# One 512-column product for a weight's upper part in the last feed-forward block of a two-model kernel

## The reference, cut to what matters

```
def sqrelu_mlp(hn, w1, w2):
    return jnp.square(jax.nn.relu(hn @ w1)) @ w2        # w1: 1024 x 4096, w2: 4096 x 1024

    hn = modulate_2(rms_norm_2(h, norm2_g[layer]), sh2, sc2)
    h = h + g2[:, None, :] * sqrelu_mlp(hn, mlp_w1[layer], mlp_w2[layer])
```

## Time and profile before

| What | Value |
|---|---|
| median of 3 runs | 1750.71 us (1750.46 to 1750.80) |
| the profiled execution, its own time | 1754.25 us |
| its span in the profile | 1752.4 us |
| mean granted TensorE clock | 0.988 of full speed |
| TensorE busy | 1679.9 us, 96% |
| VectorE busy | 1285.6 us, 73% |
| ScalarE busy | 822.3 us, 47% |
| GpSimd busy | 242.1 us, 14% |
| transfers | 317.86 MB, mean 181 GB/s |

### The profile page before, as it was taken

The page is one execution under the profiler, slowest core; times in us unless marked ns, Lnnn a source line. Parts: engine busy times, 40 slices in busy tenths (PEclk is TensorE's granted clock), DMA queues, the critical chain, the costliest instruction groups (busy, mean ns, idle before and its releaser), DMA issues.

```text
span 1752.4 us, 28651 instructions
## 1 busy us (share of the span) xinstructions
PE 1679.9 (96%) x11826; PEld 1508.6 (86%) x11826; DVE 1285.6 (73%) x1777; ACT 822.3 (47%) x1186; POOL 242.1 (14%) x199
## 2 busy tenths in 40 slices
PE   6999999999999999999999999969999999899999
PEld 3797778788788876987999999969999999799999
DVE  4667863887888878866478777887988868757453
ACT  3433662543224423646464555575635445456362
POOL 0323001011001112440310121013000220030000
PEclk9899999999999999999999999989999999999999
DMA  8644002243465558320346656634998966137552
GB/s 303 264 169 168 1 1 96 77 158 117 169 238 205 186 192 324 122 73 1 100 168 247 215 200 251 214 120 160 360 364 322 345 217 227 38 121 283 186 180 73
DMA packets 46577, 317.86 MB, mean 181 GB/s; under 512 B 5232, under 2 KB 6256, under 8 KB 12272
## 3 DMA queue, kind: packets, MB, share of 16 engines
q1 hardware_dynamic: 45936, 312.68, 49.4%
q0 software_dynamic: 512, 3.35, 0.5%
HBM read 314.96 MB, written 1.05 MB: 180 GB/s over the span
## 4 chain that ended last, share of the span: by engine, by line
PE 82%; DVE 10%; ACT 3%; issue 2%; POOL 2%; DMA 1%; DVEq 0%; ACTq 0%
PE PM L1619 22%; PE PM L1620 22%; PE PM L1621 22%; PE PO L1934 3%; PE PM L1894 2%; DVE wlo L1021 2%; PE PX L1918 2%; DVE acc L1055 1%; PE PX L1803 1%; PE PX L1592 1%; PE PX L1860 1%; DVE Hlo L1517 1%; PE PM L1703 1%; PE PX L1966 1%; PE PM L1705 1%
## 5 line engine op out<-in xcount | busy, mean ns | idle before, releaser
L1619 PE MATMUL PM<-Hhi,whi 128*128 128x256 f32 (+1 forms) x1686 | 526.9, 313 | 6.5 <-DVE Hlo L1443 2.0
L1620 PE MATMUL PM<-Hlo,whi 128*128 128x256 f32 (+1 forms) x1686 | 523.4, 310 | 0.0
L1621 PE MATMUL PM<-Hhi,wlo 128*128 128x256 f32 (+1 forms) x1686 | 523.3, 310 | 0.0
L1021 DVE TENSOR_TENSOR wlo<-raw,whi 128x2048 fp32r<-128x2048 f32 (+2 forms) x199 | 437.9, 2200 | 93.8 <-ACT whi L721 93.4
L721 ACT ACTIVATE whi<-raw 128x2048 fp32r<-128x2048 f32 (+3 forms) x204 | 365.5, 1792 | 141.8 <-PE PM L1621 91.3
L1619 PEld LDWEIGHTS PM<-Hhi,whi 128*128 128x128 f32 x1686 | 323.7, 192 | 30.1 <-issue 8.9
L1621 PEld LDWEIGHTS PM<-Hhi,wlo 128*128 128x128 f32 x1686 | 323.8, 192 | 16.4
L1620 PEld LDWEIGHTS PM<-Hlo,whi 128*128 128x128 f32 x1686 | 323.9, 192 | 15.9
L1619 PE MATMUL PM<-Ghi,whi 128*128 128x256 f32 (+1 forms) x864 | 265.1, 307 | 1.7 <-DVE X L1202 1.6
L1621 PE MATMUL PM<-Ghi,wlo 128*128 128x256 f32 (+1 forms) x864 | 263.2, 305 | 0.0
L1620 PE MATMUL PM<-Glo,whi 128*128 128x256 f32 (+1 forms) x864 | 263.2, 305 | 0.0
(11 more groups left out here) (222 smaller groups left out, 2276.4 us busy)
## 6 DMA issues: line engine op xcount, KB each, us to landing
raw<-in_ada SPq DMA_DIRECT2D x104, 1024.0 KB, 5.1
raw<-in_wm SPq DMA_DIRECT2D x93, 1024.0 KB, 5.5
raw<-in_wl SPq DMA_DIRECT2D x68, 1024.0 KB, 4.9
raw<-in_wl SPq DMA_DIRECT2D x32, 704.0 KB, 4.2
raw<-in_wm SPq DMA_DIRECT2D x5, 768.0 KB, 4.4
raw<-in_wm SPq DMA_DIRECT2D x4, 704.0 KB, 4.2
X<-in_x SPq DMA_DIRECT2D x1, 2048.0 KB, 10.9
bias<-in_bias POOLq DMA_DIRECT2D x1, 2048.0 KB, 9.8
```

What stands on the lines that cost most here:

```text
L1021: dve.tensor_tensor(wslot(wlo, i, usize(u)), slot_raw(n, usize(u)), wslot(whi, i, usize(u)).bitcast(F32), ALU.subtract)\
L1619: pe.matmul(out, st_hi, mv_hi, start=first, stop=False)
L1620: pe.matmul(out, st_hi, mv_lo, start=False, stop=False)
L1621: return pe.matmul(out, st_lo, mv_hi, start=False, stop=last)
```

## The change

It applies to 31 of the 32 MLP units of stage M1: all `w2` units and all `w1` units but index 0 (unit 172 runs in another order, with the norm before it). `Hhi` and `Hlo` become two halves of one buffer `H2`, `Ghi` and `Glo` of one buffer `G2`. For each weight block there are now two matrix multiplications: `whi` with a moving operand of two pieces of 256 columns, the upper and the lower part of the activation, into all 512 columns of a bank; and `wlo` with the upper part, 256 columns, added to the first half of that bank. The two halves of the bank are added when it is evacuated:

- `w1`: ScalarE copies the second halves to `T` (semaphore `low`); VectorE adds the first halves from PSUM (`pm_dve`), then makes max(r, 0) * r (`silu_dve`), then runs `split_lo(i + 2)`, which stood ahead of the evacuation; ScalarE makes the rounding copy into `Ghi`, VectorE the `Glo` subtraction as before.
- `w2`: VectorE does X = second half * gate + X, waits for that instruction to end, and then X = first half * gate + X.

```
+        H2 = sb("H2", 2 * KD * 512, F32R)
+        Hhi, Hlo = H2[:, 0:KD * 512], H2[:, KD * 512:2 * KD * 512]
...
+        G2 = sb("G2", 2 * HALF * 512, F32R, reg0)
+        Ghi, Glo = G2[:, 0:HALF * 512], G2[:, HALF * 512:2 * HALF * 512]
...
+        def wide(u):
+            return u["st"] == "M1" and (u["kind"] == "w2" or u["kind"] == "w1" and u["idx"] > 0)
+
+        def both_parts(u, k):
+            buf, n = (G2, HALF * 512) if u["kind"] == "w2" else (H2, KD * 512)
+            return view(buf[:, :], "p (h c) -> p h c", h=2, c=n)[:, :, k * 256:k * 256 + 256]
...
@@ ScalarE, evacuation of w1
+                    if wide(u):
+                        act.activation(view(r, "p (c t) -> p c t", c=2), view(pm(i, 0, 1024), "p (c t) -> p c t", c=2)[:, :, 256:512],
+                                       ACT.Copy).then_inc(*tick("low", i))
+                        act.wait_ge(*at("silu_dve", i))
+                        k = u["idx"] % 8
+                        act.activation(Ghi[:, k * 512:k * 512 + 512], g, ACT.Copy).then_inc(*tick("ghi", i))
+                        return
@@ VectorE, residual
+                    if wide(u):
+                        dst = X[:, c * 512:c * 512 + 256]
+                        link(dve.scalar_tensor_tensor(out=dst, in0=pm(i, 256, 256), scalar=modc(v, 0, c), in1=dst, op0=ALU.mult, op1=ALU.add))
@@ VectorE, evacuation of w1
+                    if wide(u):
+                        r, g = tslot(2 * (i % 2)), tslot(2 * (i % 2) + 1)
+                        dve.wait_ge(*at("low", i))
+                        dve.tensor_tensor(view(r, "p (c t) -> p c t", c=2), view(pm(i, 0, 1024), "p (c t) -> p c t", c=2)[:, :, 0:256],
+                                          view(r, "p (c t) -> p c t", c=2), ALU.add).then_inc(*tick("pm_dve", i))
+                        dve.wait_ge(*at("pm_dve", i))
+                        dve.scalar_tensor_tensor(out=g, in0=r, scalar=0.0, in1=r, op0=ALU.max, op1=ALU.mult).then_inc(*tick("silu_dve", i))
+                        split_lo(i + 2)
@@ VectorE, a step
-                    if (u["kind"], u["idx"]) != ("lpart", 0) and not soon:
+                    if (u["kind"], u["idx"]) != ("lpart", 0) and not soon and not (u["kind"] == "w1" and wide(u)):
                         split_lo(i + 2)
@@ TensorE, unit
+                elif wide(u):
+                    for c in range(u["cols"] // 128):
+                        for k in range(kt):
+                            if c == 0:
+                                operand_ready(u, k)
+                            w0 = k * u["cols"] + c * 128
+                            pe.matmul(view(pm(i, c * 512, 512), "p (h t) -> p h t", h=2), wslot(whi, i, 128, w0), both_parts(u, k),
+                                      start=(k == 0), stop=False)
+                            ins = pe.matmul(pm(i, c * 512, 256), wslot(wlo, i, 128, w0), mh[:, k * S:k * S + 256], start=False, stop=(k == kt - 1))
```

More of the change, by code:

```diff
@@ L346, in noted @@
         return self.known.get((name, key), 0)
-SEMAPHORES = ["small", "x_in", "hi", "lo", "raw_used", "raw_split", "unit", "pm_act", "pm_dve", "aux", "aux_act", "aux_dve",
+SEMAPHORES = ["small", "x_in", "hi", "lo", "low", "silu_dve", "raw_used", "raw_split", "unit", "pm_act", "pm_dve", "aux", "aux_act", "aux_dve",
               "silu_c", "mod", "sq", "sqadd", "sumsq", "sd", "rinv", "rspread", "xr", "hhi", "hlo", "xres",
@@ L377, in build @@
         X = sb("X", KD * 512)
-        Hhi = sb("Hhi", KD * 512, F32R)
-        Hlo = sb("Hlo", KD * 512, F32R)
+        H2 = sb("H2", 2 * KD * 512, F32R)
+        Hhi, Hlo = H2[:, 0:KD * 512], H2[:, KD * 512:2 * KD * 512]
         T = sb("T", 4 * 512)
@@ L382, in build @@
         cursor[0] += 2 * HALF * 512 * 4
-        Ghi = sb("Ghi", HALF * 512, F32R, reg0)
-        Glo = sb("Glo", HALF * 512, F32R, reg0 + HALF * 512 * 4)
+        G2 = sb("G2", 2 * HALF * 512, F32R, reg0)
+        Ghi, Glo = G2[:, 0:HALF * 512], G2[:, HALF * 512:2 * HALF * 512]
         zu = sb("zu", 2048, F32, reg0)
```

## The result

| | before | after |
|---|---|---|
| median of six runs each | 1750.59 us (1749.38 to 1752.94) | 1756.72 us (1754.38 to 1758.81) |
| ratio | | 1.0028, 95% interval 1.0017 to 1.0039 |
| the profiled execution, its span | 1754.25, 1752.4 us | 1756.82, 1755.0 us |
| unit 173's first product to the end of the span | 182.9 us | 188.3 us |
| TensorE, VectorE, ScalarE busy | 1679.9, 1285.6, 822.3 us | 1675.5, 1311.2, 813.1 us |

What follows compares the result with a forecast made beforehand. TensorE was taken as the bound, with VectorE nearly full for some 25 us. -6.6 + 6.0 + 1.0 + 0.5 + 1.7 = +2.6 us on the profiled 1754.25; median forecast 1753.3 us, range 1748.8 to 1757.0.

Steps and rivals of the forecast that it cites:

- two-piece rival: 512-column multiplication in each of 496 blocks: two-piece stream costs up to 13.3 ns a block more, 1758.8 us; chance 0.14.
- VectorE beside the ada parts: Steps 173 to 176: VectorE cycles of 6.66 or 6.96 us against TensorE's 5.55; stalls together +6.0 us.
- Stalls of 0.2, 1.4 and 4.4: TensorE waits for split_lo(176), for split_lo(177), and at the 16 sums behind unit 177 for ada part 103.
- cheap-VectorE rival: VectorE's two new instructions at 0.40 us each, so part 103 ends 2.3 us earlier: 1748.3 us; chance 0.12.
- The saving of 6.6 us: TensorE, 496 blocks of 31 units: 512 plus 256 columns take 0.3467 instead of 0.360 us, 13.3 ns less each.
- The clock: TensorE behind the 4.4 us pause: one fall of the clock to half speed, +1.7 us.
- Into w2 and the tail: First w2 units wait 0.5 us for the last Glo, twice, +1.0 us; second residual before the last store, +0.5 us.
- What the text held hidden: Loads, ScalarE's split_hi, its copy of the sums and their reader, and second residuals except at the end: no cost.

Runs made afterwards that it cites:

- narrow4: Changed kernel, but w1 units 173 to 176 keep the old three products and old evacuation; ratio to before 0.9984, stretch 181.3 us.
- interleaved: Changed kernel, but the two parts of an activation block lie side by side, so the 512-column product streams one piece; ratio 1.0036, stretch 185.3 us.
- busy_pause9: Changed kernel with 9 spare 256-column multiplications on constants ahead of the 16 sums; ratio 1.0023, stretch 186.4 us.
- lo_first: Changed kernel with split_lo(i + 2) back ahead of the evacuation in the wide w1 steps; ratio 1.0047, stretch 191.9 us.

## Why the prediction was right, and where its size was off

- **Which side.** The forecast was +2.6 us; the ratio says +4.9, the medians +6.1, the stretch +5.3. So the size forecast is about half of what came. The time, 1756.72 us, is inside the range, but only 0.3 us from its end, and that end was put there for the two-piece rival, which is not what happened: that the range held is in part luck. The likeliest class, no change within 0.2%, had 0.58, and slower, which came, 0.33.
- **VectorE beside the ada parts.** Right, and nearly to the number. Cycles of 6.66 and 6.96 were worked out, 6.59 and 6.91 measured; the forms taken for the two new instructions (0.691 and 0.692 us) were theirs. Stalls of 0.2, 1.4 and 4.4 were forecast, 0.25, 1.25 and 4.3 came, at the three places named. narrow4 shows that these four units turn the gain into a loss: without them the kernel is faster than before.
- **The cheap-VectorE rival** fell with the same rows.
- **The saving of 6.6 us** was the step that failed, by its size. The sum took "0.2267 us (as one piece)" plus 0.120 for every pair, from rows of streams with one size each. Mixed, a pair costs that or 6.7 ns more, and most pairs of this profile cost more: 4.0 us instead of 6.6. The rival that named the two-piece operand had the direction, and its price of up to 13.3 ns a block holds the 6.7, but its cause was wrong: interleaved has one piece and the same two prices. What sets the price stays open.
- **The clock.** One fall, as forecast, behind the long pause; 2.3 us instead of 1.7, and busy_pause9 shows both that the pause causes it and that it costs about 2. Part of the size is chance: in interleaved a pause of 4.02 us cost 1.7.
- **Into w2 and the tail.** 0.85 us for 1.0, and 0.52 for 0.5.
- **What the text held hidden was hidden**: loads, `split_hi`, the copy and the transposes of the sums, and the second residual of all units but the last.

The gap of 2.7 us between forecast and stretch is the pair price (+2.6) and the clock (+0.6), less 0.3 us by which the waits and the tail came out smaller: 2.9, which leaves 0.2 unexplained.

## What to carry to other kernels

An edit that takes 0.1 us a unit from the bounding engine and gives 1.4 us a unit to another has to be costed in the stage where that other one is fullest, not at its mean: 27 of 31 units gained, and four lost more than all. Look also for the wait that an engine meets in order behind a side result, for it can collect all that the other engine is behind at once; here a pause of 4.1 us also brought a spell of half speed that cost 2.3 us. A saving worked out from streams of one size is best taken as a bound when the new stream mixes sizes: here 6.6 us were worked out and 4.0 came.

## What the runs showed of the hardware that was not expected

- A stream that alternates 512- and 256-column float32r products runs at 0.3467 or 0.3533 us a pair. The price held from one break of the stream to the next (254 pairs in the change's profile, 270 in the longest, in lo_first) and could be the other one behind a break; it came with the moving data in one piece and in two. One size alone showed one price (0.120, and 0.2267 us). With 16 or 8 products of one size in a row a unit costs 5.57 or 5.59 us instead of 5.65. Why there are two prices is open.
- A pause of 0.98 us in the kernel after left the clock at 1.00, one of 4.12 us took it to 0.50, and so much work on constants that no pause was left kept it at 1.00. Pauses of 4.02 us in interleaved and 3.14 us in lo_first brought windows of 0.58 and 0.62. In lo_first the first two pairs behind the pause still took 0.45 and 0.35 us, and only after a third of 0.53 came four of 0.64: the fall can lie behind the restart. With the pauses of 1.98 us (0.60) and 2.66 us (1.00) in the kernel before, the length of a pause alone does not tell whether the clock falls.
